# Modulation slots through ScalarE and buffers of their own, and norms whose last two squares are summed on TensorE

## The reference, cut to what matters

```
c_act = silu(c)
mod = c_act @ mod_w[layer] + mod_b[layer]            # 6 vectors of 1024 a layer
u = rms_norm(h, norm_mix) * (1 + sc1) + sh1          # mix0: gated linear recurrence; mix1: chunked attention
h = h + g1 * mixer(u)
u = rms_norm(h, norm_ffn) * (1 + sc2) + sh2          # ffn0, ffn1
h = h + g2 * (silu(gate) * up) @ w_out               # u @ w_in = gate, up; width 2816
kv: k, v = split((rms_norm(h, kv_norm) * (1 + ksc) + ksh) @ kv_w)    # after layer 0
```

## Time and profile before

| | us |
|---|---|
| median of 3 runs | 2295.59 |
| lowest, highest run | 2285.57, 2300.39 |
| the profiled execution's own time | 2293.14 |
| its span, first to last instruction | 2291.3 |
| PE busy | 2157.5 (94%) |
| DVE busy | 1407.9 (61%) |
| ACT busy | 748.5 (33%) |
| POOL busy | 443.2 (19%) |
| DMA, mean over the span | 108 GB/s |

### The profile page before, as it was taken

One profiled execution on the slowest core, in us unless ns is written; L12 is line 12 of the kernel. 1 busy time (PEld: TensorE's weight loads), 2 busy tenths in 40 slices (PEclk: granted clock), 3 DMA queues, 4 the chain that ended last, 5 costly groups with the idle time before them and its releaser, 6 DMA issues.

```text
span 2291.3 us, 25604 instructions
## 1 busy us (share of the span) xinstructions
PE 2157.5 (94%) x10020; PEld 1722.6 (75%) x10020; DVE 1407.9 (61%) x1943; ACT 748.5 (33%) x963; POOL 443.2 (19%) x283
## 2 busy tenths in 40 slices
PE   6999999889999989999899999998999998999997
PEld 3787887677888867756678888876568876888885
DVE  7866765556677674377354454477556766655656
ACT  4433243322222223356332222245224234222221
POOL 3000000089988953010000000000410100000000
PEclk9999999999999998999999999999999998999998
DMA  6642321235555543221123222322013221322220
GB/s 216 209 159 93 109 94 56 74 131 208 178 189 178 181 147 129 83 101 56 56 74 109 93 93 94 108 96 68 24 56 111 92 76 72 99 97 99 93 92 37
DMA packets 39371, 248.00 MB, mean 108 GB/s; under 512 B 4927, under 2 KB 5055, under 8 KB 11348
## 3 DMA queue, kind: packets, MB, share of 16 engines
q1 hardware_dynamic: 32820, 228.91, 29.0%
q0 software_dynamic: 3088, 11.16, 1.5%
q10 hardware_dynamic: 3344, 6.29, 0.8%
HBM read 240.05 MB, written 6.29 MB: 108 GB/s over the span
## 4 chain that ended last, share of the span: by engine, by line
PE 82%; DVE 7%; issue 5%; POOL 3%; ACT 2%; DMA 1%; SPq 0%; DVEq 0%; ACTq 0%; POOLq 0%
PE bank L714 24%; PE bank L716 23%; PE bank L715 23%; PE bank L975 2%; DVE w_lo L1934 2%; PE bank L1093 1%; ACT w_hi L1441 1%; PE bank L1103 1%; PE bank L1114 1%; POOL raw L603 1%; DVE scr L1969 1%; PE bank L748 1%; DMA pool<-in_filt_w 1%; PE bank L864 1%; POOL raw L604 1%
## 5 line engine op out<-in xcount | busy, mean ns | idle before, releaser
L714 PE MATMUL bank<-u_hi,w_hi 128*128 128x512 f32 x1708 | 693.7, 406 | 38.7 <-DVE w_lo L1934 11.7
L715 PE MATMUL bank<-u_lo,w_hi 128*128 128x512 f32 x1708 | 671.2, 393 | 0.0
L716 PE MATMUL bank<-u_hi,w_lo 128*128 128x512 f32 x1708 | 671.1, 393 | 0.0
L1934 DVE TENSOR_TENSOR w_lo<-raw,w_hi 128x2048 fp32r<-128x2048 f32 x160 | 424.6, 2654 | 219.6 <-ACT w_hi L1441 219.5
L714 PEld LDWEIGHTS bank<-u_hi,w_hi 128*128 128x128 f32 x1708 | 324.5, 190 | 128.6 <-issue 48.0
L1441 ACT ACTIVATE w_hi<-raw 128x2048 fp32r<-128x2048 f32 x160 | 305.3, 1908 | 346.0 <-PE bank L716 302.9
L716 PEld LDWEIGHTS bank<-u_hi,w_lo 128*128 128x128 f32 x1708 | 324.1, 190 | 69.7
L715 PEld LDWEIGHTS bank<-u_lo,w_hi 128*128 128x128 f32 x1708 | 325.0, 190 | 66.4 <-issue 3.8
L714 PE MATMUL bank<-g_hi,w_hi 128*128 128x512 f32 x772 | 306.6, 397 | 13.4 <-DVE w_lo L1934 6.4
L716 PE MATMUL bank<-g_hi,w_lo 128*128 128x512 f32 x772 | 301.9, 391 | 0.0
L715 PE MATMUL bank<-g_lo,w_hi 128*128 128x512 f32 x772 | 301.9, 391 | 0.0
(11 more groups left out here) (293 smaller groups left out, 2229.9 us busy)
## 6 DMA issues: line engine op xcount, KB each, us to landing
raw<-in_wts SPq DMA_DIRECT2D x216, 1024.0 KB, 4.8
spectra<-pool ACTq DMA_DIRECT2D x16, 256.0 KB, 2.0
scr<-in_rel POOLq DMA_DIRECT2D x16, 256.0 KB, 3.1
pool<-spectra POOLq DMA_DIRECT2D x16, 256.0 KB, 3.1
H<-in_x ACTq DMA_DIRECT2D x1, 2048.0 KB, 24.1
out<-H SPq DMA_DIRECT2D x8, 256.0 KB, 2.0
pool<-in_filt_w POOLq DMA_DIRECT2D x2, 512.0 KB, 12.0
pool<-in_window POOLq DMA_DIRECT2D x1, 1024.0 KB, 17.5
```

Source lines behind the costliest of these rows:

```text
L714: pe.matmul(out, lh, rh, start=start, stop=False, skip_group_check=True)
L715: pe.matmul(out, lh, rl, start=False, stop=False, skip_group_check=True)
L716: return pe.matmul(out, ll, rh, start=False, stop=stop, skip_group_check=True)
L1934: dve.tensor_tensor(w_lo[RING[w]][:, :], raw[W_STREAM[w] % raw_ring][:, :], w_hi[RING[w]][:, :].bitcast(F32), ALU.subtract).then_inc(lo_do ...
```

## The change

The mods 20 to 55 leave the ring of `raw` buffers. They get three buffers `m_buf` in the arena (free in these stages), loaded by transfers that POOL starts; ACT multiplies by `c_act` in eight instructions of 128 x 256 a mod, behind the rounding of the weight slot before which the mod stood; POOL only adds. In the four norms named in `SHORT`, DVE adds six squares, and TensorE sums `ssum` and the two last squares in one accumulation of twelve matmuls. Three first slots behind a norm, and `mgate`, run as `slot_lag`, the first `mi` slot as `mlp_lead` (`slot_lag` with a lag of one, as a sequence of steps): the two matmuls with `u_hi` at chunk k, the one with `u_lo` one or two chunks late. A small `Sqrt` is put earlier in ACT's list at `ffn0`, `kv` and `ffn1`. The upper parts of `mix1` wait per half.

```
-W_STREAM = [s for s, item in enumerate(STREAM) if item[0] == "W"]
+RING_ITEMS = []
+for _s in STREAM:
+    _m += _s[0] == "M"
+    if _s[0] == "W" or _m <= M_POOLED:
+        RING_ITEMS.append(_s)
+W_STREAM = [s for s, item in enumerate(RING_ITEMS) if item[0] == "W"]
...
+SHORT = ("ffn0", "kv", "ffn1", "post2")
+ADDS = {name: 6 if name in SHORT else KC for name in MAIN}
...
+        sq_last = tn[0]
...
+        m_buf = [pool[:, a:a + SLOT] for a in (4096, 6144, 12288)]
...
+            def load_mod(m):
+                i = m - M_POOLED
+                pl.dma_start(m_buf[i % 3], A["wts"][M_SOURCE + m]).then_inc(mod_in[i % 3], 16)
...
             def sum_mods():
+                pl.wait_ge(product, READY[FIRST["wo0"]])
+                for m in range(M_POOLED, M_POOLED + 3):
+                    load_mod(m)
                 pl.wait_ge(u_l, U_FFN0 + KC)
                 for m in range(M_POOLED, NM):
-                    src = raw[s % raw_ring]
-                    pl.wait_ge(raw_in[s % raw_ring], 16 * (s // raw_ring + 1))
-                    link(pl.tensor_tensor(chunks, chunks, cact[:, :].unsqueeze(2).broadcast_to((P, KC, 256)), ALU.mult))
+                    src = m_buf[i % 3]
+                    pl.wait_ge(m_scaled, KC * (i + 1))
                     link(pl.tensor_tensor(src[:, 0:1024], src[:, 0:1024], src[:, 1024:2048], ALU.add))
...
+                    if m + 3 < NM:
+                        pl.wait_ge(m_pooled, i + 1)
+                        load_mod(m + 3)
...
+            def mlp_lead():
...
             def norm(name):
-                pe.wait_ge(sq_add, 8 * (MAIN[name] + 1))
-                norm_cols(n, ssum)
+                pe.wait_ge(sq_add, ADDED[name] + ADDS[name])
+                pe.wait_ge(*released(n - 1))
+                for x, src in enumerate((ssum, sq[0], sq_last)):
+                    if x:
+                        pe.wait_ge(sq_done, 8 * MAIN[name] + 6 + x)
+                    for j in range(TB):
+                        mm = pe.matmul(bank[6][:, j:j + 1], src[:, j * P:(j + 1) * P], onec[:, :], start=(x == 0 and j == 0),
+                                       stop=(x == 2 and j == TB - 1), skip_group_check=True)
+                mm.then_inc(n_col, 1)
                 norm_bc(n)
...
+            def slot_lag(label, i, first, count, lag, nout=2):
+                w, hi, lo = weights(label, i)
+                banks = [claim(first + j) for j in range(nout)]
+                for k in range(KC + lag):
+                    if k < KC:
+                        pe.wait_ge(u_h, count + k + 1)
+                        for j in range(nout):
+                            c = k * 256 + j * P
+                            pe.matmul(banks[j][:, :], hi[:, c:c + P], u_hi[:, k, :], start=(k == 0), stop=False, skip_group_check=True)
+                            pe.matmul(banks[j][:, :], lo[:, c:c + P], u_hi[:, k, :], start=False, stop=False, skip_group_check=True)
+                    if k >= lag:
+                        x = k - lag
+                        wait_u(count + x + 1)
...
-                            slot_std(f"fi{layer}", i, FIRST[f"fi{layer}_{i}"], ucount)
+                            if i:
+                                slot_std(f"fi{layer}", i, FIRST[f"fi{layer}_{i}"], ucount)
+                            else:
+                                slot_lag(f"fi{layer}", i, FIRST[f"fi{layer}_{i}"], ucount, 2)
...
+            slot_lag("kk", 0, FIRST["kk"], U_KV, 2)
+            for i in range(1, 4):
...
+            slot_lag("qq", 0, FIRST["qq"], U_MIX1, 2)
...
+            slot_lag("mgate", 0, FIRST["mgate"], U_PRE2, 1, nout=1)
...
-            lead = mlp_slot(0)
+            lead = mlp_lead()
...
+            def scale_mod(m):
+                i = m - M_POOLED
+                act.wait_ge(mod_in[i % 3], 16 * (i // 3 + 1))
+                for k in range(KC):
+                    x = m_buf[i % 3][:, k * 256:(k + 1) * 256]
+                    act.activation(x, x, ACT.Identity, bias=zcol[:, 0:1], scale=cact[:, k:k + 1]).then_inc(m_scaled, 1)
...
                     act.activation(w_hi[RING[w]][:, :], raw[s % raw_ring][:, :], ACT.Copy).then_inc(hi_done, 1)
+                    for m in range(M_POOLED, NM):
+                        if M_BEFORE[m] == w:
+                            scale_mod(m)
...
+            def root_table(name):
+                act.activation(rt[:, 8 + MAIN[name]:9 + MAIN[name]], zcol[:, 1:2], ACT.Sqrt)
...
-            modulated("mix1", U_MIX1, SC1_1, SH1_1, lambda c: used("vv", 3))
+            modulated("mix1", U_MIX1, SC1_1, SH1_1, lambda c: used("vv", 2 + c // 4))
...
-                    if c:
+                    if 1 <= c < KC - 2:
                         add_square("ffn0", c - 1)
+            add_square("ffn0", KC - 3)
```

More of the change, by code:

```diff
@@ L453, in build @@
         rel_ready, mask_ready, taps_in = sem("rel_ready"), sem("mask_ready"), sem("taps_in")
+        m_scaled = sem("m_scaled")
+        mod_in = [sem(f"mod_in{x}") for x in range(3)]
         w4_in, row_done, row_out = sem("w4_in"), sem("row_done"), sem("row_out")
@@ L560, in _ @@
             w = m = 0
-            for s, item in enumerate(STREAM):
+            for s, item in enumerate(RING_ITEMS):
                 if s >= raw_ring:
@@ L853, in mlp_slot @@
                     yield
+            def mlp_lead():
+                w, hi, lo = weights("mi", 0)
+                banks = [claim(FIRST["mi0"] + j) for j in range(2)]
+                for k in range(KC + 1):
+                    if k < KC:
+                        pe.wait_ge(u_h, U_MLP + k + 1)
+                        for j in range(2):
+                            c = k * 256 + j * P
+                            pe.matmul(banks[j][:, :], hi[:, c:c + P], u_hi[:, k, :], start=(k == 0), stop=False, skip_group_check=True)
+                            pe.matmul(banks[j][:, :], lo[:, c:c + P], u_hi[:, k, :], start=False, stop=False, skip_group_check=True)
+                    if k:
+                        wait_u(U_MLP + k)
+                        for j in range(2):
+                            c = (k - 1) * 256 + j * P
+                            mm = pe.matmul(banks[j][:, :], hi[:, c:c + P], u_lo[:, k - 1, :], start=False, stop=(k == KC),
+                                           skip_group_check=True)
+                            if k == KC:
+                                complete(mm, FIRST["mi0"] + j, w if j else None)
+                    yield
             def norm_cols(n, src):
@@ L1396, in _ @@
             norm("post2")
-            lead = mlp_slot(0)
+            lead = mlp_lead()
             follow = mlp_slot(1)
-            for k in range(KC):
+            for k in range(KC + 1):
                 next(lead)
@@ L1457, in squares @@
                     act.wait_ge(*finished(name, c))
-                    if 8 * MAIN[name] + c >= 2:
-                        act.wait_ge(sq_add, 8 * MAIN[name] + c - 1)
-                    act.activation(sq[c % 2], src[:, c, :], ACT.Square).then_inc(sq_done, 1)
+                    last = name in SHORT and c == KC - 1
+                    if c >= 2 and not last:
+                        act.wait_ge(sq_add, ADDED[name] + c - 1)
+                    elif c < 2 and name != "mix0":
+                        ahead_of = next(x for x in MAIN if MAIN[x] == MAIN[name] - 1)
+                        if ahead_of in SHORT:
+                            act.wait_ge(n_col, NORM[ahead_of] + 1)
+                        else:
+                            act.wait_ge(sq_add, ADDED[name] + c - 1)
+                    act.activation(sq_last if last else sq[c % 2], src[:, c, :], ACT.Square).then_inc(sq_done, 1)
+            def root_table(name):
+                act.activation(rt[:, 8 + MAIN[name]:9 + MAIN[name]], zcol[:, 1:2], ACT.Sqrt)
             def root(n):
@@ L1624, in _ @@
                 ahead("wo0", i)
+                if i == 0:
+                    root_table("ffn0")
                 squares("ffn0", H, (2 * i, 2 * i + 1))
@@ L1711, in _ @@
                 ahead("wo1", i)
+                if i == 0:
+                    root_table("ffn1")
                 squares("ffn1", H, (2 * i, 2 * i + 1))
@@ L2235, in ffn @@
                                 after(c - 1)
[L2237 removed]
             factors(NORM["ffn0"])
             modulated("ffn0", NORM["ffn0"], U_FFN0, SC2_0, SH2_0)
[L2240 to L2243 removed]
+            ffn("0", G_FFN0, 0, G2_0, "wo0", lambda c: c < ADDS["kv"] and add_square("kv", c))
             factors(NORM["kv"])
```

48 lines of the change are left out of this document (26 added, 22 removed).

## The result

The kernel after takes 2271.89 us (median of 4 runs, 2269.25 to 2277.35) against 2297.99 for the kernel before, run beside it: ratio 0.9904, 95% interval 0.9875 to 0.9932. Measured again with the experiments it took 2272.61 (ratio 0.9904, 0.9887 to 0.9921). The kernel before had medians of 2293.94, 2293.91 and 2293.09 there, over 20, 11 and 11 runs, so the gain is about 21.5 us. The forecast of 2271 lies 1 us off, and in part that is luck: the forecast gain of 24.35 us is some 3 more than the measured one, and it was taken from a median of 2295.59 that lies 2 above the later ones. The experiments show that parts of the forecast were wrong in opposite directions: the mods alone bring 24.6 us, where 20 was forecast, and the edits at the norms and at the MLP's first slot, forecast at +4.3, come out at a loss of about 3, within overlapping intervals.

The account below looks back on a forecast made before the run. TensorE, busy 94% of the span, was taken as the bound. Terms 15 + 5.05 - 2.0 + 3.9 + 0.4 + 2.0 = 24.35 us off 2293.14 gave 2268.8, and 2271 as median; range 2256 to 2286.

Parts of the forecast that it names:

- The mods: First FFN: taking the mods from the raw ring wins 15 us, ceiling 16.6, or 6.1 if POOL's time alone counts.
- the hole is the ring's: First FFN: TensorE's 6.82 us wait for one `w_lo` comes from held `raw` buffers; ring alone as cause would win 16.6.
- ACT's scalings and POOL's loads: Weight slots: scalings of 4.3 us a mod and loads landing within 23 us stay hidden, cost 0.
- The norm `kv`: Norm `kv`: DVE's adds no longer slowed by POOL's multiplication, 5.05 us won, bounds 4 to 5.9.
- Two squares on TensorE: Four norms: columns start 1.4 us earlier but 16 more instructions run, 0.5 us lost each, -2.0 in all.
- Late lower parts: Behind norms `ffn0`, `kv`, `ffn1`: TensorE starts at the first `u_hi`, 1.3 us earlier each, 3.9 won, bounds 2 to 4.5.
- `mix1`: At `mix1`: one `u_lo`, 0.74 us, less waiting, and less low clock behind it, 2.0 us won, bounds 0.7 to 2.2.
- `mlp_lead`: MLP's first slot: one `u_lo`, 0.74 us, less idle time before its second chunk: 0.4 us won, bounds 0 to 0.75.
- `mgate` and the root's table: `mgate`, where TensorE has no wait, and the square root's table load, already hidden: each wins 0.
- the columns cost more than forecast: Rival, chance 0.25: the norms' 24 column instructions at half clock cost 7.2 us more, the FFN keeps some 4: 2282.
- the loads were not late: Rival, chance 0.06: POOL's loads land after 23 us, delaying ACT's `w_hi` and TensorE; 2348 us at a 30 us landing.
- the clock did not hold: Rival, chance 0.14: TensorE stays at 2.4 GHz in some norms, some 2.5 us each; 2261 us.

Follow-up runs that it names:

- experiment 1: The kernel after, but POOL multiplies each mod again in the mod's own buffer and ACT's eight scalings go: 2293.43 us, ratio 1.0 to the kernel before.
- experiment 2: The kernel after, but mods stay in the raw ring, where ACT scales them and POOL only adds: 2285.04 us, ratio 0.9959 to the kernel before.
- experiment 4: The kernel after again, 2272.61 us; mods only plus the two squares on TensorE, 2273.73; mods only plus late lower parts in four places, 2267.30.
- experiment 6: The kernel after with lower parts right behind each upper chunk at the four `slot_lag` places: 2272.10 us, ratio 0.9915 to the kernel before.
- mods only: The kernel after with only its modulation part (eight adds, plain first slots, no early root table, old `mix1` bound): 2269.34 us, ratio 0.9891 to before.
- experiment 5: Against the kernel after: eight adds a norm, 2269.20 us; plain first MLP slot, 2272.25; both, 2266.93; second MLP slot one chunk later, 2272.99.

## Why the prediction came out right, and which steps did not

**The mods, forecast 15 of at most 16.6: measured 17.8.** All of it came. The ceiling took 0.51 us a mod for the column sums that stay; what stays is 14.7 in all, 0.46 a mod. But the reason given failed: "the hole is the ring's", with the ring alone worth up to 16.6. The ring alone is worth 6.1 in the FFN, and nothing in the kernel's time (experiment 1). The lower bound, 6.1 for POOL's time alone, was met by 5.9 (experiment 2). What the working missed is that either cause is sufficient to keep most of the loss: with a held ring, weights come late once, when POOL starts; with a free ring and the multiplication on POOL, a sum comes late there and DVE's additions at the stage's end. It also kept POOL's additions at 6.36 us a mod; they fell to 4.6.

**ACT's scalings and POOL's loads, forecast 0.** Held: 4.0 us a mod, landing 5.2 us, no wait of PE behind them. The Trainium skill, "SBUF — State Buffer", section "Who interferes with whom", warned of loads started by GpSimd beside VectorE in its two-port modes; no run here shows such a delay, 5.2 us against 4.9 for SP's.

**The norm `kv`, forecast 5.05: measured 5.1** (17.4 to 12.28 with the mods alone). The add of two tiles took 4.11 us beside POOL in experiment 1, and the row between two such adds, which reads one tile from a PSUM bank, 0.74 as ever. The Trainium skill, "SBUF — State Buffer", section "Who interferes with whom", says that a VectorE instruction with two SBUF inputs contends with a GpSimd instruction that reads SBUF; the trace agrees, with these 4.11 us against 0.68 for the same add without POOL (kernel after, 835.87 us).

**Two squares on TensorE, forecast -2.0: -2.6 or -4.0 in the stages, -4.4 between the medians of experiment 4.** Mechanism right: 1.4 us less idle time ahead of the columns, 24 instead of 8 of them. The term was mis-sized: 24 take 2.84 to 4.69 us, and the clock falls among them, at three of the four norms, rather than after them.

**Late lower parts, forecast 3.9: 2 to 3.** At the norms 2.7 by the pair in experiment 4 (10.61, 12.28 and 10.73 to 10.24, 11.08 and 9.62), 3.5 by experiment 6, and 3.7 from mods only to the kernel with both undone of experiment 5 (9.42, 11.11 and 9.41). So the term held at the norms, nearly; the first FFN behind gives 0.6 of it back in that kernel (377.0 us against 376.42) and 1.1 in the one of experiment 4.

**`mix1`, forecast 2.0: 0.8.** The idle time fell from 2.17 to 1.39 us, one `u_lo`. The further 1.2 for a clock that would hold did not come from the edit. The low stretch of the earlier trace rows at `mix1` is gone in the kernel after, but it is in mods only too, which has none of these edits, and a low stretch of the same length stands 18 us later, at a wait of 2.5 us:

```profile
941.70:945.20 3.50, 3.47 (x15) 2.92 (x16) 3.50 (x6) 2.56 (x4) 0.00 (x0) 1.00 0.02 5
959.90:963.30 3.40, 3.40 (x10) 1.47 (x9) 1.47 (x7) 1.09 (x4) 0.00 (x0) 0.50 0.70 255
```

The per-half bound is worth 0, as forecast: with the late lower parts and without the bound (experiment 4) the stretch from the last product of `vv` to the first of `qq` is 1.77 us, with both 1.78.

**`mlp_lead`, forecast +0.4: -3.3 in the MLP.** The step that failed by its sign. The slot does start sooner: the norm `post2` takes 11.41 us, and 12.20 with the plain slot. The working looked at how much sooner the slot starts, and not at when it ends: its lower parts now run one chunk late, the last of them behind a chunk of the second slot, and `mi0`'s end releases the next weights. That the slot's end is what sets the hole is shown by experiment 5. Of the loss, 1.8 us is idle time at the hole, in each profile with this slot, and the rest the low clock behind it, which varies. With `post2` counted in, the slot costs 3.0 us against the plain one in the kernel after and 0.4 with eight adds.

**`mgate` and the root's table, forecast 0.** The last kernel of experiment 5 and the mods with late lower parts differ by the root's table and the bound of `mix1` alone: 2266.93 and 2267.30 us, no difference. No run tried `mgate` alone.

So the sum, 24.35 forecast and some 21.5 measured, comes out near because the mods brought 4.6 more than their two terms and the rest 7 less: two errors that partly cancel, which is luck. Of the rivals none came true as a whole: the columns cost more than forecast, but the FFN kept nothing of its loss; the loads were not late; the clock did not hold (at `kv` the low stretch fell from 20.5 and 17.1 us to 13.7, at `ffn1` it stayed 10.2); and the FFN's loss went.

## What to carry to other kernels

When a stage loses to two resources at once (a buffer held too long and an engine that works too long while holding it), price each with the other still in place; here each alone gave 6 us and both 18. Look also for where in the stage the waits lie: here what was left of them with one resource freed lay at its start and end, and not in the 300 us between. An instruction moved earlier or later within a slot is priced at the slot's last use of its buffer, not at its start. An edit worth 1 to 3 us at a point where TensorE idles anyway is below what these runs resolve; read it from its stage in two profiles, and expect the neighbouring columns or the clock to take part of it.

## What the runs showed of the hardware that was not expected

In the first FFN of the kernel before, DVE and POOL lengthen each other's instructions. POOL's addition of 128 x 1024 takes 2.40 us where it meets no DVE instruction with both tensors in SBUF (7 of 33) and up to 4.33 where it does. DVE's `w_lo` takes 2.28 us where it meets no POOL instruction (2 of 33), and 3.98 on the mean and up to 5.40 where it does. Its instruction that reads one tensor from a PSUM bank (L2023) takes 0.74 in either case (22 and 65). The buffer is not the reason: in experiment 2 POOL adds in the ring's buffers, and its three additions take 2416, 1347 and 799 ns, as in the kernel after (2398, 1347 and 802).

The low stretches of TensorE's clock come and go at places where neither code nor data differ: 444.99 and 451.48 us for the same first stage of the same kernel, and 266.79 against 271.82 for the same attention stretch, the longer one with low stretches of 6.8 us at 980 us and 3.4 at 1117 that the other lacks. Runs of one kernel lie 1 to 17 us apart, and "mods only", the calmest, 1.0.
